# Rotary and memory-attention keys stored twice beside zeros, so that their score matmuls use all 128 rows

## The reference, cut to what matters

```
q_pe = apply_rope(rms_norm(q_mla[..., MLA_NOPE:], g_q_rope), cos, sin)
k_pe = apply_rope(rms_norm(k_rope, g_k_rope)[:, :, None, :], cos, sin)
q_full = jnp.concatenate([q_nope, q_pe], axis=-1)
k_full = jnp.concatenate([k_nope, jnp.broadcast_to(k_pe, (B, S, MLA_HEADS, MLA_ROPE))], axis=-1)
o_mla = causal_block_attention(q_full, k_full, v_mla, (MLA_NOPE + MLA_ROPE) ** -0.5)
...
s_m = jnp.einsum('bshd,bmhd->bhsm', q_m, k_m).astype(jnp.float32) * (MEM_DQK ** -0.5)
```

## Time and profile before

| | |
|---|---|
| median of 3 runs | 963.65 us (963.45 to 965.89) |
| profiled execution, span from first to last instruction | 962.8 us |
| TensorE matmul busy | 948.7 us, 99% |
| VectorE busy | 719.2 us, 75% |
| ScalarE busy | 224.3 us, 23% |
| GpSimd busy | 23.5 us, 2% |
| chain that ended last, by engine | TensorE 87%, VectorE 10%, ScalarE 2% |
| L2225 (latent attention, 64 rows) | 32 MATMUL records, 9.5 us |
| L2264 (memory attention, 64 rows) | 16 MATMUL records, 4.5 us |

### The profile page before, as it was taken

How to read it: one execution, slowest core, us unless ns; L and a number is a source line. 1 busy time by engine, 2 the same in 40 slices (tenths; PEclk the granted TensorE clock), 3 DMA queues, 4 the chain that set the end, 5 groups by cost and what they waited for, 6 DMA issues and landing times.

```text
span 962.8 us, 12510 instructions
## 1 busy us (share of the span) xinstructions
PE 948.7 (99%) x4998; PEld 588.8 (61%) x4998; DVE 719.2 (75%) x1260; ACT 224.3 (23%) x442; POOL 23.5 (2%) x27
## 2 busy tenths in 40 slices
PE   7999999999999999999999999999999999999998
PEld 6944445755555458999844459447854444468544
DVE  4875964578967887966899863988968689674667
ACT  4313412223231223422200011201012221434100
POOL 0000000000002500000000000000000000000000
PEclk9999999999999999999999999999999999999999
DMA  9551831434434524344444434423424443321631
GB/s 334 147 197 34 293 131 44 175 106 158 158 128 125 174 104 168 131 176 175 175 175 175 174 123 141 175 88 114 150 88 175 160 147 141 130 80 45 223 127 45
DMA packets 51770, 139.76 MB, mean 145 GB/s; under 512 B 3968, under 2 KB 7904, under 8 KB 51712
## 3 DMA queue, kind: packets, MB, share of 16 engines
q1 hardware_dynamic: 50256, 135.07, 39.9%
q0 software_dynamic: 1248, 3.80, 1.5%
q10 hardware_dynamic: 208, 0.08, 0.0%
HBM read 137.90 MB, written 1.05 MB: 144 GB/s over the span
## 4 chain that ended last, share of the span: by engine, by line
PE 87%; DVE 10%; ACT 2%; issue 1%; DMA 0%; DVEq 0%; ACTq 0%
PE pair L2041 30%; PE pair L2126 20%; PE pair L2122 16%; DVE arena L974 6%; PE pair L2383 6%; PE turned L1986 3%; PE score L2383 3%; PE turned L2383 1%; PE score L2550 1%; PE score L2478 1%; PE score L2225 1%; DVE ring L974 1%; PE score L2224 1%; PE score L2563 1%; DVE arena L1254 1%
## 5 line engine op out<-in xcount | busy, mean ns | idle before, releaser
L2041 PE MATMUL pair<-ring,hT 128*128 128x512 f32 (+2 forms) x512 | 213.6, 572 | 0.9 <-ACT hT L622 0.9
L974 DVE TENSOR_TENSOR arena<-arena 128x256 f32<-128x256 f32 (+6 forms) x332 | 196.7, 607 | 17.2 <-PE score L2383 4.1
L2041 PEld LDWEIGHTS pair<-ring,hT 128*128 128x128 f32 x512 | 95.3, 190 | 102.6 <-issue 97.7
L2126 PE MATMUL pair<-ring,arena 128*128 128x512 f32 x192 | 85.8, 594 | 0.0
L2126 PE MATMUL pair<-ring,hT 128*128 128x512 f32 x184 | 84.0, 597 | 1.0 <-DMA ring<-in_w_in 1.0
L2126 PE MATMUL pair<-arena 128*128 128x512 f32 x176 | 79.8, 595 | 0.1
L974 DVE TENSOR_TENSOR arena<-pair,arena 128x512 f32<-128x512 f32 x60 | 41.5, 692 | 49.9 <-PE pair L2126 26.0
L2041 PE MATMUL pair<-hT,ring 128*128 128x128 f32 (+2 forms) x464 | 76.2, 324 | 0.2 <-ACT hT L622 0.2
L974 DVE TENSOR_TENSOR arena<-ring 128x2048 f32<-128x2048 f32 (+1 forms) x39 | 72.3, 1854 | 2.7 <-DMA ring<-in_w_ssm_out 1.4
L2041 PEld LDWEIGHTS pair<-hT,ring 128*128 128x128 f32 (+1 forms) x464 | 66.0, 188 | 8.6 <-ACT hT L622 1.0
L2122 PE MATMUL pair<-arena 128*128 128x128 f32 x544 | 64.0, 276 | 0.0
(11 more groups left out here) (226 smaller groups left out, 1012.1 us busy)
## 6 DMA issues: line engine op xcount, KB each, us to landing
ring<-in_w_in SPq DMA_DIRECT2D x33, 2048.0 KB, 8.4
ring<-in_w_up SPq DMA_DIRECT2D x8, 2048.0 KB, 8.4
ring<-in_w_down SPq DMA_DIRECT2D x8, 2048.0 KB, 8.0
ring<-in_w_o SPq DMA_DIRECT2D x4, 2048.0 KB, 7.9
ring<-in_w_mem_kv SPq DMA_DIRECT2D x2, 2048.0 KB, 8.0
ring<-in_w_glu SPq DMA_DIRECT2D x2, 2048.0 KB, 7.8
ring<-in_w_ssm_out SPq DMA_DIRECT2D x2, 2048.0 KB, 7.8
ring<-in_w_ukv SPq DMA_DIRECT2D x4, 512.0 KB, 3.8
```

The lines of the kernel that those rows point to most:

```text
L974: return dve.tensor_tensor(o, a, b, op)
L2041: ins = pe.matmul(o_, s, m, start=a, stop=b)
L2126: ins = pe.matmul(h[bank_], rows[:, k, :], weights[:, k, :], start=not onto and k == 0, stop=k == 3, skip_group_check=True)
```

## The change

`kpeT` becomes 512 columns wide. Its columns 0 to 255 hold the rotated key in partitions 0 to 63 and zeros in 64 to 127; columns 256 to 511 hold zeros above and the key below. A head's rotary score now takes all 128 partitions of `qpT` (its own query and its neighbour's) against the half of `kpeT` where the neighbour meets zeros. In memory attention the keys of even heads go to the upper half of the old `kmT` place and the keys of odd heads to the lower half of `kpeT`, each beside 64 rows of zeros. GpSimd writes the zeros with four memsets; ScalarE copies each transposed key tile with two activations of 64 partitions (`turned_keys`) in place of one of 128. TensorE waits on a new semaphore `key_zero` before each of the two loops. `kpeT` is 256 columns longer, so what is placed after it in that arena moves by 256 columns.

```diff
-        kmT, qmT = qpT[:, 0:512], qpT[:, 512:1024]
         knT = a1(2048); o_mem = knT
-        kpeT = a1(256)
+        kpeT = a1(512)
+        kmT, qmT = (qpT[:, 0:512], kpeT), qpT[:, 512:1024]
...
+            pool.memset(kpeT[64:128, 0:SEQ], 0.0).then_inc(sem("key_zero"), 1)
+            pool.memset(kpeT[0:64, SEQ:2 * SEQ], 0.0).then_inc(sem("key_zero"), 1)
             pool.wait_ge(sem("weights2"), 16)
...
             for n, i in enumerate(GATES):
+                if n == 2:
+                    pool.wait_ge(sem("mla_scores"), MH)
+                    pool.memset(kmT[0][64:128, :], 0.0).then_inc(sem("key_zero"), 1)
+                    pool.memset(kmT[1][0:64, 0:SEQ], 0.0).then_inc(sem("key_zero"), 1)
...
+            def turned_keys(halves, n):
+
+                i = n_turn[0]
+                n_turn[0] += 1
+                act.wait_ge(sem("turned_ready"), i + 1)
+                for e, dst in enumerate(halves):
+                    r = slice(64 * e, 64 * e + 64)
+                    ins = act.activation(dst[r, :], bank["turned"][i % 2][r, 0:n], ACT.Copy)
+                ins.then_inc(sem("turned_taken"), 1)
...
-            turned(kpeT, 256)
+            turned_keys((kpeT[:, 0:SEQ], kpeT[:, SEQ:2 * SEQ]), SEQ)
...
-                    turned(kmT, 512)
+                    turned_keys(kmT, 512)
...
             is_turned("kn")
-
+            pe.wait_ge(sem("key_zero"), 2)
...
-                    r = slice(64 * (h % 2), 64 * (h % 2) + 64)
...
-                        ins = pe.matmul(o, qpT[r, SEQ * (h // 2) + P * t:SEQ * (h // 2) + P * t + P], kpeT[r, 0:w], start=False, stop=True)
+                        ins = pe.matmul(o, qpT[:, SEQ * (h // 2) + P * t:SEQ * (h // 2) + P * t + P], kpeT[:, SEQ * (h % 2):SEQ * (h % 2) + w],
+                                        start=False, stop=True)
...
             is_turned("km")
+            pe.wait_ge(sem("key_zero"), 4)
...
-                    r = slice(64 * (i % 2), 64 * (i % 2) + 64)
                     for t in range(TT):
-                        ins = pe.matmul(b[:, SEQ * t:SEQ * t + SEQ], qmT[r, SEQ * (i // 2) + P * t:SEQ * (i // 2) + P * t + P],
-                                        kmT[r, SEQ * (i // 2):SEQ * (i // 2) + SEQ], start=True, stop=True)
+                        ins = pe.matmul(b[:, SEQ * t:SEQ * t + SEQ], qmT[:, SEQ * (i // 2) + P * t:SEQ * (i // 2) + P * t + P],
+                                        kmT[i % 2][:, SEQ * (i // 2):SEQ * (i // 2) + SEQ], start=True, stop=True)
```

More of the change, by code:

```diff
@@ L180 @@
     "x_rows": "normalised tiles of x", "mem_rows": "normalised tiles of the memory", "ckv_rows": "tiles of the latent",
-    "kpe_rows": "rotated key, twice", "q_rows": "queries without rotation", "qpe_rows": "rotated queries",
+    "kpe_rows": "rotated key, twice", "key_zero": "GpSimd: zeros beside the rotated key, then beside the memory's keys", "q_rows": "queries without rotation", "qpe_rows": "rotated queries",
     "k_rows": "keys without rotation", "m_rows": "memory attention's queries, then keys",
```

## The result

The changed kernel takes 958.98 us in the median of 5 runs (958.53 to 960.21) against 964.44 us for the kernel before in the same rounds (5 runs). The ratio is 0.9945, with a 95% interval of 0.9935 to 0.9956: 0.5% faster, 5.5 us.

What follows compares the result with a forecast made beforehand. TensorE was taken to bound the kernel, except VectorE from 221.46 to 262 us. Span 962.8 - 5.9 (latent scores) + 0.1 (second copy) = 957.0 us, with 0.85 us around it 957.9 us; range 956.3 to 960.3 us.

Steps and rivals of the forecast that it cites:

- What bounds the kernel: Whole span: TensorE's list sets the time, 87% of the chain, except where VectorE does, from 221.46 to 262 us.
- Latent attention's scores: Eight heads' score matmuls: without passages between 128 and 64 rows, 0.73 us saved a head, 5.9 us in all.
- the rival of operands and banks: Same as A: score passages cost through changed operands or adding into one bank, not 64 rows; no saving, 5%.
- VectorE and the weights follow: Heads of latent attention: VectorE's 2.13 us wait and the weight load's 4.2 us spare let the full 5.9 us through.
- C: Rival, 20 us ahead of 221 us: something other than TensorE starts VectorE, half the gain lost; 960.5 us, 8%.
- ScalarE's second copy: Copy of `km` ahead of the sigmoid: 0.5 us longer, covered by VectorE's 0.57 us wait; at most 0.1 us lost.
- Memory attention's scores: Four memory heads: 1.2 us shorter on TensorE, but inside VectorE's stretch, so 0 gained; bounds 0 and 1.2 us.
- GpSimd's memsets and the shift: Four zeroing memsets and the arena's 256-column move: counted as nothing; for the shift, a tenth either way.
- From span to time: Around the profiled span: 0.85 us added to the 957.0 us span, giving a time of 957.9 us.
- A: Rival, latent scores: the saving does not exist, 64 rows not being the cause; 963.6 us, 5%.
- B: Rival, memory attention: its scores' 1.2 us gain gets through as well; 956.7 us, 8%.
- D: Rival, VectorE's stretch: TensorE's longer idle time sets its clock back to 1.2 GHz, slower; 967 us, 1 to 2%.

Runs made afterwards that it cites:

- e1: Changed kernel with memory attention's keys, their copy and matmuls put back as before, so latent attention alone is changed; 959.47 us, ratio 0.994.
- e3: Kernel before with each head's two 128-row score products first and its two 64-row ones after, two passages instead of four; 961.53 us, ratio 0.9969.
- e4: Changed kernel with latent attention's rotary score matmuls cut to partitions 0 to 95; 959.66 us in a single run.
- e2: Changed kernel with latent attention put back as before, so only memory attention's keys stand beside zeros; 965.23 us, ratio 1.001.
- e7: Changed kernel with ScalarE's sigmoid between its two copies of the memory's keys and GpSimd zeroing `amat` in VectorE's place; 957.65 us, ratio 0.9935 to before.
- e5: Kernel before with the place of `kpeT` made 256 columns longer and nothing else; 964.11 us, ratio 1.0003.
- e6: Kernel before plus GpSimd's two early 64x256 memsets and ScalarE waiting for them, no shift; 964.01 us, ratio 1.0002.
- e8: e6 plus two long-fulfilled waits on `key_zero` in TensorE's list; 964.68 us, ratio 1.0002 to before.
- e9: Changed kernel with its two `key_zero` waits moved from TensorE to ScalarE; 957.72 us, ratio 0.9938 to before.
- e11: Kernel before with GpSimd zeroing `amat` in VectorE's place; 963.99 us, ratio 0.9996.
- e0: Kernel before run once more, unchanged, for a second profile; 963.97 us.
- e10: e7 with the two `key_zero` waits moved from TensorE to ScalarE; 956.99 us, ratio 0.9924 to before.

## Why the prediction was right, and where it missed

- What bounds the kernel: right. TensorE's list through the heads, VectorE from 221 to 262 us.
- Latent attention's scores, 5.9 us: right. The turn went from 3.04 to 2.31 us (eight times that is 5.84 us; 5.89 us were measured between the first score and turn 8), e1 has the gain alone, e3 half of it. Its cause, the passages between 64 and 128 rows, held against the rival of operands and banks: the changed kernel and e4 keep the banks, the order and the alternation of operands, and only the row count is another. The single passages are not alike: the first entry of a turn costs 0.09 us, the second 0.20 us.
- VectorE and the weights follow: right, with 0.91 and 1.50 us of VectorE's waits left in the turns of heads 6 and 7. The sentence under C that VectorE runs without a pause from 199.31 us on misreads its own rows: VectorE waits 1.39 us at 219.66 us for the sigmoid.
- ScalarE's second copy, taken at 0.5 us and, behind its cover, at no more than 0.1 us: it is 0.73 us, and 0.18 us come out. The estimate took the distance of two copies of one kind as the price of one more; two halves last 1.18 us where one copy lasted about 0.6.
- Memory attention's scores, 0 us: right (e1, e2). The waits grew to 2.2 us, as forecast. The 1.2 us by which the list is shorter are right too, though the share is not 0.3 us for each head: from the product ahead of the scores to what stands behind them e7 saves 0.34 to 0.35 us in three heads and 0.20 us in the first, where the column form changes to 128*32 right behind the scores in both kernels.
- GpSimd's memsets and the shift, nothing: right. The shift is e5 and the early memsets are e6. The later pair takes 0.52 and 0.30 us at 189 us and was not tried alone; in e2, with one early memset and this pair, nothing is lost between the first score and the end beyond the 0.2 us of the split copy.
- The waits on `key_zero`: I asked only whether they are fulfilled in time, and wrote that TensorE's list keeps its instructions. It has two more. They are fulfilled in time and cost 0.5 to 1.0 us all the same in most executions, outside the span (e8, e9).
- From span to time: I took 0.85 us from a span and a median that did not belong to the same execution. It is 1.87 us without the waits and 2.4 to 2.9 us with them. The profiled execution of before must itself have taken near 964.7 us (an estimate, 962.8 + 1.87), not the 963.65 us it was paired with. The time was forecast at 957.9 us and came out at 958.98 us. That median execution has a span of 956.2 us and 2.78 us outside: what lies around the span was taken 1.9 us too small and the span 0.8 us too large, and the two partly cancel. The mis-sized term is what lies around the span. That the profiled execution's span, 957.3 us, came so near the forecast 957.0 us is in part luck, since the spans of the five executions lie between 955.8 and 957.3 us.

The rivals: A (no saving) is ruled out by the distances in head 7's turn, B (the memory part counts) and C (half is lost) by the shift of 5.47 us at 262 us (C was priced at 960.5 us, though the range that is said to reach to it ends at 960.3 us), and the granted clock stayed full in all five executions, so D did not happen. Its mechanism exists, at another place: in e3 the clock fell behind the weight wait near 109 us.

## What to carry to other kernels

Look for matmuls of 64 rows that stand alone between matmuls of 128: here each pair of changes cost 0.34 to 0.39 us, with matmuls 128 and 256 wide in between, and zeros in the other half take them out; the small matmuls side by side leave one pair (e3). A shorter list in a stretch that another engine sets gives nothing until that engine's list is shorter too; then both gains come together (e7). Compare times with times and spans with spans: close to a microsecond can lie outside the span, because of instructions that wait for nothing. And where the start of a program varies, measure a small gain from a fixed event behind it to the end: that showed half a microsecond in e11 that ten timed executions did not.

## What the runs showed of the hardware

- 96 rows between matmuls of 128 rows cost nothing, 64 rows cost 0.34 to 0.39 us for the pair of changes (e3, e4).
- A ScalarE copy of 64 partitions x 512 lasts as long as one of 128 x 512: 1.18 us for two, against 0.60 us for the one; alone they take 0.58 and 0.59 us (e7).
- Waits in TensorE's list that were long fulfilled moved the last packet of the instruction queue from inside the span to 1.7 to 1.8 us after the last instruction, and put 0.5 to 1.0 us outside the span in most executions (e6 against e8, e9).
- The wait for weights near 109 us changes from execution to execution between 0.7 and 2.0 us with the same code ahead of it, but 0 to 0.6 us of it come out: from the transposes ahead of it to the first score it is 30.05 us in before and e0 (waits of 0.96 and 0.70 us) and 30.64 us after (1.96 us). Most of the spread of the spans is there by the first large product, which starts at 11.48 us (e6, span 961.2 us), 12.41 us (e0, 962.1 us) or 13.06 us (before, 962.8 us); behind the first score these three differ by less than 0.1 us.
- The granted clock fell to 0.68 in the 5.3 us behind such a wait of 1.97 us in e3, and the product there took 5.24 us in place of 3.53; behind waits of 1.96 us in the profiles of after and e10 it stayed full.
